# Running the first inversion level of a gated DeltaNet block on 32x32 quarters

## What is computed

```python
a = jnp.where(strict, jnp.einsum('bhnld,bhnsd->bhnls', k_beta, k) * decay, 0.0)
rhs = jnp.concatenate([v * beta[..., None], k_beta * jnp.exp(g_cum)[..., None]], axis=-1)
sol = lax.linalg.triangular_solve(a, rhs, left_side=True, lower=True, unit_diagonal=True)
```

## Time and profile before

| | |
|---|---|
| median of 3 runs | 2890.29 us |
| the profiled execution: device time | 2888.65 us |
| the profiled execution: first to last instruction (span) | 2886.9 us |
| TensorE busy | 2817.2 us, 98% of the span |
| VectorE, ScalarE, GpSimd busy | 54%, 48%, 3% |
| share of the chain that ended last | PE 85%, DVE 7%, ACT 4% |
| L771 (128x128 by 128), x704 records | 69.7 + 14.9 us busy |
| L780 (64x64 by 64), x384 records | 25.7 us busy |

### The profile page before, as it was taken

How to read it: one execution, slowest core, us unless ns; L and a number is a source line. 1 busy time by engine, 2 the same in 40 slices (tenths; PEclk the granted TensorE clock), 3 DMA queues, 4 the chain that set the end, 5 groups by cost and what they waited for, 6 DMA issues and landing times.

```text
span 2886.9 us, 36757 instructions
## 1 busy us (share of the span) xinstructions
PE 2817.2 (98%) x13396; PEld 2326.4 (81%) x13396; DVE 1561.2 (54%) x1934; ACT 1373.9 (48%) x1874; POOL 96.2 (3%) x67
## 2 busy tenths in 40 slices
PE   8999999999999999999999999999999999999998
PEld 6788788888888888887878787887888888888886
DVE  4554665544545455557585757655454454544444
ACT  5354545444444344455665657454444444444443
POOL 0000000000000000001010101000000000000000
PEclk9999999999999999999999999999999999999999
DMA  7464466666666666644353535555566666666664
GB/s 235 145 201 148 140 192 186 189 189 189 189 189 189 190 189 189 197 137 143 108 161 105 154 117 154 155 159 188 185 189 191 189 189 189 189 190 188 205 192 143
DMA packets 261264, 502.66 MB, mean 174 GB/s; under 512 B 20112, under 2 KB 20368, under 8 KB 260624
## 3 DMA queue, kind: packets, MB, share of 16 engines
q1 hardware_dynamic: 259504, 494.67, 57.3%
q10 hardware_dynamic: 816, 3.15, 0.3%
q0 software_dynamic: 816, 3.15, 0.3%
HBM read 495.65 MB, written 5.24 MB: 174 GB/s over the span
## 4 chain that ended last, share of the span: by engine, by line
PE 85%; DVE 7%; ACT 4%; issue 1%; DVEq 1%; ACTq 0%; DMA 0%; SPq 0%
PE acc L545 26%; PE acc L539 26%; PE acc L540 26%; PE aux L771 2%; DVE wlo L1397 2%; PE aux L592 2%; DVE const L1758 1%; DVE arena L1796 1%; ACT whi L967 1%; PE aux L780 1%; DVE arena L1793 1%; DVE arena L1758 1%; ACT arena L1313 0%; DVEq L1762 0%; PE aux L744 0%
## 5 line engine op out<-in xcount | busy, mean ns | idle before, releaser
L1397 DVE TENSOR_TENSOR wlo<-wraw,whi 128x1024 fp32r<-128x1024 f32 x928 | 1145.3, 1240 | 1142.3 <-ACT whi L967 1133.7
L967 ACT ACTIVATE whi<-wraw 128x1024 fp32r<-128x1024 f32 x928 | 973.7, 1060 | 1094.3 <-PE acc L545 1038.8
L539 PE MATMUL acc<-whi,hT_hi 128*128 128x512 f32 x2624 | 1040.0, 396 | 7.5 <-ACT whi L967 7.1
L540 PE MATMUL acc<-whi,hT_lo 128*128 128x512 f32 x2624 | 1024.4, 390 | 0.0
L545 PE MATMUL acc<-wlo,hT_hi 128*128 128x512 f32 x2624 | 708.5, 392 | 25.0 <-DVE wlo L1397 24.5
L545 PEld LDWEIGHTS acc<-wlo,hT_hi 128*128 128x128 f32 x2624 | 490.2, 188 | 142.9 <-DVE wlo L1397 42.0
L539 PEld LDWEIGHTS acc<-whi,hT_hi 128*128 128x128 f32 x2624 | 494.0, 188 | 109.4 <-issue 7.9
L540 PEld LDWEIGHTS acc<-whi,hT_lo 128*128 128x128 f32 x2624 | 494.1, 188 | 100.7 <-issue 1.0
L539 PE MATMUL acc<-whi,arena 128*128 128x512 f32 x1088 | 427.4, 393 | 3.2 <-ACT whi L967 3.2
L540 PE MATMUL acc<-whi,arena 128*128 128x512 f32 x1088 | 425.1, 391 | 0.0
L545 PE MATMUL acc<-wlo,arena 128*128 128x512 f32 x1088 | 293.4, 392 | 0.0
(11 more groups left out here) (234 smaller groups left out, 1191.0 us busy)
## 6 DMA issues: line engine op xcount, KB each, us to landing
wraw<-in_l_w_in SPq DMA_DIRECT2D x304, 512.0 KB, 3.8
wraw<-in_l_w_gate SPq DMA_DIRECT2D x176, 512.0 KB, 3.7
wraw<-in_l_w_up SPq DMA_DIRECT2D x176, 512.0 KB, 3.7
wraw<-in_l_w_down SPq DMA_DIRECT2D x176, 512.0 KB, 4.0
wraw<-in_l_w_out SPq DMA_DIRECT2D x96, 512.0 KB, 4.6
o_rounds<-arena POOLq DMA_DIRECT2D x3, 1024.0 KB, 4.7
arena<-o_rounds ACTq DMA_DIRECT2D x3, 1024.0 KB, 6.1
x<-in_x SPq DMA_DIRECT2D x4, 512.0 KB, 6.0
```

The costliest lines, as they stand in the source:

```text
L539: nc.tensor.matmul(pair[m], hi[:, k, tok], wh, start=first, stop=False)
L540: nc.tensor.matmul(pair[m], lo[:, k, tok], wh, start=False, stop=False)
L967: nc.scalar.activation(whi[:, s, :], wraw[:, s, :], ACT.Copy).then_inc(hi_done, 1)
L1397: V.tensor_tensor(wlo[:, s, :], wraw[:, s, :], whi[:, s, :].bitcast(F32), ALU.subtract).then_inc(lo_done, 1)
```

## The change

Level 32 no longer works on whole 128 x 128 matrices. In such a matrix only the two blocks (rows 1, columns 0) and (rows 3, columns 2) of 32 x 32 change. `level_q` now takes these blocks directly from `A_` (no `B32`, no `level_part`, no mask among the constants) and multiplies them with 32 x 32 diagonal blocks of `TT`: 16 matmuls a chunk. `level_t` computes both the new blocks of `TT` (right half of the chunk's PSUM area) and the one of `T` that is used later (left half): 24 matmuls a chunk. Both chunks have half of `aux[1]` each, the pair `halves`, so they no longer take turns. VectorE writes the new blocks with the sign turned (6 instructions of 32 partitions) in place of subtracting. The steps move: level 32 is in steps 23 and 24, `last_q` in 27, `last_tt` in 28.

```diff
             def gdn(r):
                 pool.wait_ge(a_set, D_AT(r, 1))
-                level_part()
                 nc.gpsimd.memset(TT[:], 0.0).then_inc(tt_zero, 1)
...
-                for b in range(4):
+                for b in range(3):
...
-                def level_q(c, to):
-                    per_head(to, lambda h: B32[:, c, h, :], lambda h: TT[:, c, h, :]).then_inc(lev_psum, 1)
...
+                def level_q(c, to):
+
+                    for h in range(HV):
+                        for b in (0, 2):
+                            mm = nc.tensor.matmul(to[quarter(b), h * LEAF:(h + 1) * LEAF], A_[quarter(b + 1), c, h, quarter(b)],
+                                                  TT[quarter(b + 1), c, h, quarter(b + 1)], start=True, stop=True)
+                    mm.then_inc(lev_psum, 1)
+
                 def level_t(c, to):
-                    quarters(to, lambda h: Q1[0:HALF, c, h, 0:HALF], lambda h: T[0:HALF, c, h, 0:HALF])
+
+                    for h in range(HV):
+                        for b in (0, 2):
+                            nc.tensor.matmul(to[quarter(b), 256 + h * LEAF:256 + (h + 1) * LEAF], T[quarter(b), c, h, quarter(b)],
+                                             Q32[quarter(b), c, h, :], start=True, stop=True)
+                        mm = nc.tensor.matmul(to[quarter(1), h * LEAF:(h + 1) * LEAF], Q32[quarter(0), c, h, :],
+                                              T[quarter(0), c, h, quarter(0)], start=True, stop=True)
+                    mm.then_inc(lev_psum, 1)
...
                 if s == 23:
                     pe.wait_ge(et_copy, D_AT(r, 1))
-                    pe.wait_ge(part_set, PART_AT(r, 0))
                     pe.wait_ge(tt_in, r + 1)
-                    level_q(0, aux[1])
+                    level_q(0, halves[0])
+                    level_q(1, halves[1])
                 if s == 24:
-                    pe.wait_ge(part_set, PART_AT(r, 1))
-                    pe.wait_ge(lev_copy, LEVEL_COPY(r, "q32_0"))
-                    level_q(1, aux[1])
                     pe.wait_ge(conv_sum, TOK_AT(r, Q))
                     token_major(Q, aux[0])
+                    pe.wait_ge(t_in, r + 1)
+                    for c in range(M):
+                        pe.wait_ge(lev_copy, LEVEL_COPY(r, f"q32_{c}"))
+                        level_t(c, halves[c])
                 if s == 25:
-                    pe.wait_ge(t_in, r + 1)
-                    pe.wait_ge(lev_copy, LEVEL_COPY(r, "q32_1"))
-                    level_tt(0, aux[1])
                     pe.wait_ge(tok_copy, TOK_AT(r, Q))
                     products(0, aux[0])
                 if s == 26:
-                    pe.wait_ge(lev_sub, LEVEL_SUB(r, "TT32_0"))
-                    level_t(0, aux[1])
                     pe.wait_ge(gram_mask, GRAM_AT(r, "kq"))
                     conv_transposes(V1, aux[0])
                 if s == 27:
-                    pe.wait_ge(lev_sub, LEVEL_SUB(r, "T32_0"))
-                    level_tt(1, aux[1])
+                    for c in range(M):
+                        pe.wait_ge(lev_sub, LEVEL_SUB(r, f"T32_{c}"))
+                        last_q(c, halves[c])
                 if s == 28:
-                    pe.wait_ge(lev_sub, LEVEL_SUB(r, "TT32_1"))
-                    level_t(1, aux[1])
...
-                if s == 29:
-                    pe.wait_ge(lev_sub, LEVEL_SUB(r, "T32_1"))
-                    last_q(0, halves[0])
-                    last_q(1, halves[1])
+                    for c in range(M):
+                        pe.wait_ge(lev_copy, LEVEL_COPY(r, f"q64_{c}"))
+                        last_tt(c, halves[c])
                 if s == 30:
-                    pe.wait_ge(lev_copy, LEVEL_COPY(r, "q64_0"))
-                    last_tt(0, halves[0])
-                    pe.wait_ge(lev_copy, LEVEL_COPY(r, "q64_1"))
-                    last_tt(1, halves[1])
                     pe.wait_ge(conv_sum, TOK_AT(r, V1))
                     token_major(V1, aux[0])
...
+                def level_new(c):
+
                     dve.wait_ge(lev_psum, LEVEL_PSUM(r, f"T32_{c}"))
-                    changed = T[0:HALF, c, :, 0:LEAF]
-                    V.tensor_tensor(changed, changed, quarter_of(aux[1][0:HALF, 0:NB])[:, :, 0:LEAF], ALU.subtract).then_inc(lev_sub, 1)
+                    src = aux[1][:, c * NB:(c + 1) * NB].rearrange("p (e h n) -> p e h n", e=2, n=LEAF)
+                    V.tensor_scalar(TT[quarter(0), c, :, quarter(1)], src[quarter(0), 1], -1.0, None, ALU.mult)
+                    V.tensor_scalar(TT[quarter(2), c, :, quarter(3)], src[quarter(2), 1], -1.0, None, ALU.mult)
+                    V.tensor_scalar(T[quarter(1), c, :, quarter(0)], src[quarter(1), 0], -1.0, None, ALU.mult).then_inc(lev_sub, 1)
```

More of the change, by code:

```diff
@@ L58 @@
 GW = (8, 64)
-LEVELS = [32]
 HALF = P // 2
 CONST_PARTS = [("ident", 128), ("upto", 128), ("after", 128), ("ones", 128), ("neg", 384),
-               ("low_up", 256), ("levels", 128 * len(LEVELS)), ("decay", RH * 256), ("freq", 128),
+               ("low_up", 256), ("decay", RH * 256), ("freq", 128),
                ("leaf_eye", LEAF * LEAF // 2)]
@@ L89, in shape_constants @@
     put("low_up", np.concatenate([a > b, a <= b], 1))
-    put("levels", np.concatenate([((a // (2 * n)) == (b // (2 * n))) & ((a // n) % 2 == 1) & ((b // n) % 2 == 0)
-                                  for n in LEVELS], 1))
     i, half = np.arange(LEAF)[None, :, None], np.arange(LEAF // 2)[None, None, :]
@@ L162 @@
 LEAF_AT = counts("T", "TT")
-PART_AT = counts(0, 1)
-LEVEL_PSUM = counts("q32_0", "q32_1", "TT32_0", "T32_0", "TT32_1", "T32_1", "q64_0", "q64_1", "TT64_0", "TT64_1")
+LEVEL_PSUM = counts("q32_0", "q32_1", "T32_0", "T32_1", "q64_0", "q64_1", "TT64_0", "TT64_1")
 LEVEL_COPY = counts("q32_0", "q32_1", "q64_0", "q64_1")
-LEVEL_SUB = counts("TT32_0", "T32_0", "TT32_1", "T32_1", "TT64_0", "TT64_1")
+LEVEL_SUB = counts("T32_0", "T32_1", "TT64_0", "TT64_1")
 END_PSUM = counts("vn0", "s", "o0", "ks", "qs", "vn1", "o1")
@@ L267, in build @@
         leaf_TT = at(86 * KB, [P, M * HV, LEAF])
-        Q1 = at(84 * KB, [P, M, HV, P])
+        Q32 = at(88 * KB, [P, M, HV, LEAF])
         Q64 = at(84 * KB, [P, M, HV, HALF])
@@ L339, in build @@
         t_in = sem("t_in")
-        part_set = sem("part_set")
         k_tail_set = sem("k_tail_set")
@@ L825, in gdn @@
                     conv_transposes(Q, aux[0])
+                halves = [aux[1][:, c * NB:(c + 1) * NB] for c in range(M)]
                 if s == 23:
                     pe.wait_ge(et_copy, D_AT(r, 1))
-                    pe.wait_ge(part_set, PART_AT(r, 0))
                     pe.wait_ge(tt_in, r + 1)
-                    level_q(0, aux[1])
+                    level_q(0, halves[0])
+                    level_q(1, halves[1])
                 if s == 24:
-                    pe.wait_ge(part_set, PART_AT(r, 1))
-                    pe.wait_ge(lev_copy, LEVEL_COPY(r, "q32_0"))
-                    level_q(1, aux[1])
                     pe.wait_ge(conv_sum, TOK_AT(r, Q))
                     token_major(Q, aux[0])
+                    pe.wait_ge(t_in, r + 1)
+                    for c in range(M):
+                        pe.wait_ge(lev_copy, LEVEL_COPY(r, f"q32_{c}"))
+                        level_t(c, halves[c])
                 if s == 25:
-                    pe.wait_ge(t_in, r + 1)
-                    pe.wait_ge(lev_copy, LEVEL_COPY(r, "q32_1"))
-                    level_tt(0, aux[1])
                     pe.wait_ge(tok_copy, TOK_AT(r, Q))
@@ L1222, in value_rows, with level_copy @@
                     a.then_inc(tok_copy, 1)
-                def level_copy(step, c, src):
-                    act.wait_ge(lev_psum, LEVEL_PSUM(r, step))
-                    nc.scalar.activation(Q1[:, c].rearrange("p h n -> p (h n)"), src[:, :], ACT.Copy).then_inc(lev_copy, 1)
+                def level_copy(step, dst, rows, cols):
+                    for c in range(M):
+                        act.wait_ge(lev_psum, LEVEL_PSUM(r, f"{step}_{c}"))
+                        nc.scalar.activation(dst[0:rows, c].rearrange("p h n -> p (h n)"), aux[1][0:rows, c * NB:c * NB + cols], ACT.Copy
+                                             ).then_inc(lev_copy, 1)
                 if s == 0:
@@ L1270, in gdn @@
                 if s == 23:
-                    act.wait_ge(t_in, r + 1)
-                    level_copy("q32_0", 0, aux[1])
+                    level_copy("q32", Q32, 3 * LEAF, HV * LEAF)
                     silu(Q)
                 if s == 24:
-                    level_copy("q32_1", 1, aux[1])
                     act.wait_ge(tok_tr, TOK_AT(r, Q))
@@ L1283, in gdn @@
                     load_o(2)
+                if s == 27:
+                    act.wait_ge(t_in, r + 1)
+                    level_copy("q64", Q64, HALF, HV * HALF)
                 if s == 29:
[L1285 to L1288, removed]
                     silu(V1)
@@ L1844, in gdn @@
                     conv(Q)
+                if s == 24:
```

(9 more changed lines are left out.)

7 lines of the change are left out of this document (removed).

## The result

The changed kernel takes 2863.82 us (median of 4 runs, 2861.21 to 2864.72) against 2891.1 us for the kernel before (2888.48 to 2892.19, 4 runs): ratio 0.9905, 95% interval 0.9891 to 0.9919, so 27.3 us less. The forecast was 20 us less. The miss that counts is the 6.7 us to the forecast of 2870.5. A second set of runs of the same kernel gave 2863.84 us.

The account below looks back on a forecast made before the run. TensorE, busy 98%, was taken as the bound: 6.45 us less from unit 25 to 31, minus 1.52 for its later start, gives 4.9 a round, 19.7 in four; 2868.95 us, 2870.5 on the median's footing. Range 2864 to 2884.

Parts of the forecast that it names:

- the price of a record at 32: Level 32 matmuls in steps 23 and 24: 0.0315 us a record, two records per fp32 matmul, 160 a round.
- The line from 128 and 64: Straight line through 0.111 us a record at 128 and 0.058 at 64, giving 0.0315 at 32; chance 0.50 with near it.
- The rule on parallel tiles: Skill page on TensorE: different tiles can load and multiply in parallel; cited as what would give rival 2.
- The rule on the floor: Skill page on TensorE: about 60 cycles overhead per matmul, making 32 columns as dear as 64, 0.058 us a record.
- rival 2: Level 32 matmuls in different quarters overlap, two at once: 0.016 us a record, -25.7 us, 2864.8 us; chance 0.12.
- -7.96: Round's change on TensorE at record price p: -7.96 + 96p us, plus 64p - 2.42 if positive.
- The cover in step 23: `level_q`'s 0.47 us of extra time vanishes in unit 24's 0.87 us wait for `wlo`, which VectorE delivers late.
- The 0.23 for both changes of shape: On TensorE, going to the small matmul shape and back costs 0.23 us, added once each in steps 23 and 24.
- Level 32 on VectorE: Six new instructions of 32 x 256 replace four subtractions: 0.48 us each by the nearest row, 2.9 us in all.
- the masked copies: GpSimd loses its masked copies; it is busy 3%, so nothing is gained or lost.
- Rival 1: A floor: level 32 records cost as much as at 64, 0.058 us; -4.4 us, 2886 us; chance 0.17.
- rival 3: Going from quarter to quarter costs in every level 32 matmul: 0.089 us a record, +15.4 us, 2906 us; chance 0.06.

Follow-up runs that it names:

- the grouped order: The changed kernel with its level 32 matmuls ordered one place at a time instead of alternating; 2872.29 us, run again for a profile 2871.96 us.
- the split kernel: The changed kernel with 4 of 12 instructions of VectorE's convolution of Q moved to step 22 and `level_t` ahead of the transposes; 2863.65 us.
- the two halves: The changed kernel with level 64's chunk 1 writing partitions 64 to 127 and both chunks alternating head by head; 2856.21 us.
- halves and split: The changed kernel with both level 64's chunks alternating between output halves and the split convolution of Q with `level_t` ahead of the transposes; 2853.23 us.
- the fourth place: The changed kernel with a fourth matmul per head in `level_t`, rows 2 to output quarter 3, result unread; 2862.77 us.
- the mask early: The kernel of halves and split with VectorE's mask on `products` moved from step 25 to step 24; 2852.27 us.

## Why the prediction was wrong, and what of it held

| term, per round | forecast | measured, round 0 |
|---|---|---|
| `level_q` with the return (64 records) | 2.25 us | 1.13 us |
| unit 24's `wlo` group starts at | 1354.96 | 1354.95 |
| transposes of Q | 0.85 us | 0.96 us |
| `level_t` with the return (96 records) | 3.25 us | 1.14 us |
| unit 25 starts, against before | +1.52 us | -0.47 us |
| unit 25 to unit 31 | 24.6 us | 24.43 us |
| sum | -4.9 us | -7.1 us |

**The step that failed** is the price of a record at 32, 0.0315 us for all 160 records. Measured were 0.0160 in `level_q` and 0.0107 in `level_t`, because neighbouring matmuls of different places ran together. Of this only `level_t`'s part reached the time, 2.1 us a round, since the wait for `wlo` covers `level_q`'s. The line from 128 and 64 down to 0.0315 us was right for one place. What failed was to sum with it for every record, and to give the overlap of places a chance of only 0.12. The rows could not decide it, since all groups of the earlier trace rows write to one half, as the text said; a tie in the rows is no reason for a small chance. The rule on parallel tiles that the text cited (the Trainium skill, TensorEngine Tiling (Array Packing), Key Properties) agrees with the pace of `level_q` and `level_t`. The rule on the floor (the Trainium skill, TensorEngine Tiling (Array Packing), Instruction Overhead) does not show: at one place a record of 32 columns takes 0.0315 us, about half of the 0.058 at 64.

**The range** missed for a second reason. Its low end was rival 2 with two places in turn, 0.016 for all 160 records. The diff shows three places per head in `level_t`, and 0.0315 / 3 = 0.0105 there gives -7.96 + 96 x 0.0105 = -6.95 a round, 2862.5 us. The mechanism was named, and its size was not counted out from the code. The measured -7.1 differs from that by the 0.17 of steps 25 to 30, and the execution adds up: 2888.65 - 28.7 + 1.4 = 2861.35 us, against 2861.21. The 1.4 at the output projection stand in no term of the forecast; without them the miss of the range would be larger, so it is small by luck. Two slips changed nothing: rival 2's own sum is 2890.29 - 25.7 = 2864.6 us, not 2864.8, and the "three" waits in steps 23 to 30 are four as listed.

**What held.** The cover in step 23: `level_q`'s saving of 0.65 us against before moved unit 24 forward and went wholly into its wait for `wlo`, 0.70 before and 1.31 now; the grouped order showed the same cover from the other side. The 0.23 for both changes of shape: about 0.12 on the way back, and the 0.11 that the transposes ahead of `level_t` take over their 0.85 fits the way there. `TT`'s quarters are the only wait ahead of the three new lines (0.37). Nothing waits ahead of `last_q` or `last_tt`. Level 32 on VectorE was cheaper than its bound, and the masked copies were worth nothing. Rival 1 (a floor) and rival 3 (a price for each change of place) are ruled out: a record that changes place costs less than one that stays.

**What stays open** is the clock. It fell in step 23, in or right behind `level_q`, in 3 of 4 rounds of the grouped order's profile, 3 of 4 with level 64 back in its steps, 2 of 4 of the split kernel, 1 of 4 with the two halves, 1 of 4 with halves and split, and in none of 8 in the two profiles of the changed kernel, nor of 4 with the fourth place or with the mask early. The grouped order's 5 us beyond its own cost fit that. Four of the kernels in which it fell keep the alternating order, so the grouping is not needed for a fall. But falls go with it: the mean granted share of an execution is 0.993 or less in 9 of the 10 executions of the grouped order (its tenth, at 0.995, took 2865.52 us) and in 8 of the 32 of the eight other runs with the new level 32 (these have the alternating order). By what way the order acts on the clock is not shown, and neither is the cause of the fall at the output projection.

## What to carry to other kernels

Price small matmuls by place: pace of one place (here 0.058 us a record at 64, 0.032 at 32) times records, divided by the number of places with other output partitions that consecutive matmuls go through (other rows alone were not run). Count the places in the code before setting the ends of a range, and let matmuls that now write to one half alternate between halves (here 0.93 us for every 32 records). A saving ahead of a group that is late for another engine is not gained, so look for what holds that engine, and then for what its moved work makes late in turn.

## What was not expected of the hardware

- Matmuls that share the rows of the array and differ only in output partitions overlap fully: 0.034 us a record at 64 x 64 with the return in two halves (1.08 / 32) against 0.063 in one (2.01 / 32), and a pair every 32 ns at 32 x 32.
- Four places at 32 x 32 take a record every 8.8 ns, so neither the issue of load and matmul nor the writes of four matmuls into one chunk's PSUM area held them up visibly at that pace.
- The return from the small shape to the units costs about 0.12 us after 32 x 32 (1.13 less 1.01), about half of the 0.23 for both ways.
- The granted clock can drop to half behind a wait or a stretch of small matmuls, and two kernels can differ in this at the same place: share 0.50 behind `level_q` in the grouped order, 0.50 behind the wait of 3.15 us at the output projection, where the kernel before kept 1.00. Executions of one kernel differ in how much: mean share 0.992 to 0.996 over the eight of the changed kernel, whose two profiles agree in where (half clock from 1464.3 and 1955.8 us in one, from 1463.9 and 1955.4 in the other).
